# First scores inside the last projection job of three attention layers, and three moved steps

## What is computed

```python
# layer 1 (moba_attention; one block of 256 keys, so it is causal softmax attention, 8 heads)
proj = h @ w_in                       # 10 column blocks of 512, the last four through a sigmoid
p = softmax(q @ k.T * scale, causal); y = p @ v
# layer 4 (odd_mixer, 16 heads)
q, k, v = split(h @ w_qkv, 3); q = rms_norm(q, q_norm); k = rms_norm(k, k_norm)
p = softmax(q @ k.T * scale + bias); y = (p @ v) @ w_out
# layer 6 (fox_mixer, 16 heads)
log_f = log_sigmoid(f + b_f); c = cumsum(log_f)          # the forget sums
p = softmax(q @ k.T * scale + c[q] - c[k], causal); y = ((p @ v) * silu(z)) @ w_out
# layer 7 (nsa_mixer): attention on compressed blocks, then two more branches
p_c = softmax(q @ kc.T * scale); o_c = p_c @ vc          # the compressed weights are p_c
```

## Time and profile before

| What | Value |
|---|---|
| Time, median of 3 runs (lowest to highest) | 2000.18 us (2000.02 to 2001.02) |
| Time of the profiled execution | 1999.24 us |
| Its span | 1997.5 us |
| Mean granted clock of TensorE | 0.996 of 2.4 GHz |
| Busy: PE, PE weight loads, DVE, ACT, POOL | 1933.7, 1592.1, 1522.3, 1272.0, 96.2 us |
| Chain that ended last: PE, DVE, ACT, DMA, issue | 85%, 7%, 4%, 2%, 2% |
| DMA | 535.14 MB, mean 268 GB/s |

### The profile page before, as it was taken

How to read it: one execution, slowest core, us unless ns; L and a number is a source line. 1 busy time by engine, 2 the same in 40 slices (tenths; PEclk the granted TensorE clock), 3 DMA queues, 4 the chain that set the end, 5 groups by cost and what they waited for, 6 DMA issues and landing times.

```text
span 1997.5 us, 26032 instructions
## 1 busy us (share of the span) xinstructions
PE 1933.7 (97%) x9572; PEld 1592.1 (80%) x9572; DVE 1522.3 (76%) x1718; ACT 1272.0 (64%) x1400; POOL 96.2 (5%) x102
## 2 busy tenths in 40 slices
PE   6999999999998999999999999999999989999998
PEld 4887887888887788888888888888888867778876
DVE  7666766544586789989898988989989884467686
ACT  4544676534545677777787777877777765446464
POOL 1000300000000320000000000000000000100001
PEclk9999999999999999999999999999999999999999
DMA  9863645555452599999999999999999995624500
GB/s 366 275 226 120 213 169 191 203 183 189 159 193 82 180 412 367 377 387 365 385 356 392 370 381 376 373 388 358 380 387 370 377 366 169 211 64 149 174 1 32
DMA packets 186269, 535.14 MB, mean 268 GB/s; under 512 B 12609, under 2 KB 23893, under 8 KB 186198
## 3 DMA queue, kind: packets, MB, share of 16 engines
q1 hardware_dynamic: 179952, 518.95, 71.0%
q10 hardware_dynamic: 4422, 8.92, 1.2%
q0 software_dynamic: 1824, 6.31, 1.1%
HBM read 521.02 MB, written 13.12 MB: 267 GB/s over the span
## 4 chain that ended last, share of the span: by engine, by line
PE 85%; DVE 7%; ACT 4%; DMA 2%; issue 2%; ACTq 0%; DVEq 0%; SPq 0%
PE bank L467 25%; PE bank L469 24%; PE bank L468 24%; DVE WL L1193 3%; ACT WH L1189 2%; PE bank L671 1%; DMA ring<-in_od_we_down 1%; PE bank L660 1%; PE bank L2772 1%; DVE P L1177 1%; PE bank L375 1%; PE bank L439 1%; PE bank L686 1%; PE bank L684 1%; DMA ring<-in_od_we_up 1%
## 5 line engine op out<-in xcount | busy, mean ns | idle before, releaser
L1193 DVE TENSOR_TENSOR WL<-ring,WH 128x2048 fp32r<-128x2048 f32 x475 | 1073.0, 2279 | 257.6 <-ACT WH L1189 254.0
L1189 ACT ACTIVATE WH<-ring 128x2048 fp32r<-128x2048 f32 x475 | 901.8, 1912 | 351.0 <-PE bank L469 332.0
L467 PE MATMUL bank<-WH,XTH 128*128 128x512 f32 (+1 forms) x1872 | 738.3, 394 | 9.2 <-DVE XTL L396 3.0
L469 PE MATMUL bank<-WH,XTL 128*128 128x512 f32 (+1 forms) x1872 | 727.8, 389 | 0.0
L468 PE MATMUL bank<-WL,XTH 128*128 128x512 f32 (+1 forms) x1872 | 727.1, 388 | 0.0
L467 PEld LDWEIGHTS bank<-WH,XTH 128*128 128x128 f32 x1872 | 352.6, 188 | 95.0 <-DVE WL L1193 14.7
L469 PEld LDWEIGHTS bank<-WH,XTL 128*128 128x128 f32 x1872 | 352.5, 188 | 73.5
L468 PEld LDWEIGHTS bank<-WL,XTH 128*128 128x128 f32 x1872 | 353.0, 189 | 68.8 <-issue 0.2
L467 PE MATMUL bank<-WH,HTH 128*128 128x512 f32 (+1 forms) x568 | 219.9, 387 | 1.4 <-DVE WL L1193 1.1
L469 PE MATMUL bank<-WH,HTL 128*128 128x512 f32 (+1 forms) x568 | 217.9, 384 | 0.0
L468 PE MATMUL bank<-WL,HTH 128*128 128x512 f32 (+1 forms) x568 | 217.6, 383 | 0.0
(11 more groups left out here) (450 smaller groups left out, 1382.2 us busy)
## 6 DMA issues: line engine op xcount, KB each, us to landing
ring<-in_od_we_gate SPq DMA_DIRECT2D x112, 1024.0 KB, 7.2
ring<-in_od_we_up SPq DMA_DIRECT2D x112, 1024.0 KB, 8.5
ring<-in_od_we_down SPq DMA_DIRECT2D x112, 1024.0 KB, 8.4
ring<-in_w_in SPq DMA_DIRECT2D x20, 1024.0 KB, 6.8
ring<-in_fox_w_in SPq DMA_DIRECT2D x16, 1024.0 KB, 6.6
ring<-in_nsa_w_in SPq DMA_DIRECT2D x14, 1024.0 KB, 5.0
ring<-in_w_ada SPq DMA_DIRECT2D x12, 1024.0 KB, 10.3
ring<-in_ev_w_in SPq DMA_DIRECT2D x12, 1024.0 KB, 5.2
```

The costliest lines, as they stand in the source:

```text
L467: nc.tensor.matmul(out, x[0], wt[0][:, k, :], start=start, stop=False, skip_group_check=check)
L469: return nc.tensor.matmul(out, x[1], wt[0][:, k, :], start=False, stop=stop, skip_group_check=check)
L1189: nc.scalar.activation(wh, slot_ap(n, nk, width), ACT.Copy).then_inc(hi_made, 1)
L1193: nc.vector.tensor_tensor(wl, slot_ap(n, nk, width), wh.bitcast(F32), ALU.subtract).then_inc(lo_made, 1)
```

## The change

- `Project` gets `shift`, which turns the four banks by two; P1 uses it. Job 9 then writes banks 0 and 1, job 8 banks 2 and 3.
- In layers 1, 4 and 6 the scores of pair 0 are issued between the two halves of the last job (keys (9, 1, 0), (5, 1, 0) and (8, 1, 0)). DVE does `highest` of units 0 and 1 behind the splits of the last job and ahead of its wait for the eviction; ACT does the exponentials of units 0 and 1 ahead of the eviction of the last job. PE's wait for all evictions moves: in layers 1 and 6 behind the scores of pair 2 (scores of pair 1 wait for the last but one job), in layer 4 behind the turns of units 0 and 1, ahead of the scores of pair 1.
- Layer 4: queries are turned ahead of the second half of job 4, keys inside the first half of job 5 (ahead of token tile 1). ACT evicts the query turns and takes the root for the keys ahead of the eviction of job 4, and evicts the key turns and rounds the router weights behind it; DVE evicts the query turns ahead of the norm of the keys. `roped` is raised once more, so later waits on it count one more. In A4 the transposes for the output product come one step sooner (`soon=1`).
- Layer 6: DVE copies the forget sums ahead of its wait for the eviction of job 4 instead of behind it.
- Layer 7: the turn of the compressed weights moves from ahead of the second half of job 7 to ahead of that half's token tile 1.

```diff
@@ -472,15 +472,15 @@
...
-    def __init__(self, jobs, lhs, scale=None, narrow=None, tall=None, by_parts=0):
-        self.jobs, self.lhs, self.scale, self.by_parts = jobs, lhs, scale, by_parts
+    def __init__(self, jobs, lhs, scale=None, narrow=None, tall=None, by_parts=0, shift=0):
+        self.jobs, self.lhs, self.scale, self.by_parts, self.shift = jobs, lhs, scale, by_parts, shift
...
-        return bank[4 + tt if c == 2 and self.by_parts == 3 else (2 * c + tt) % 4]
+        return bank[4 + tt if c == 2 and self.by_parts == 3 else (2 * (c + self.shift) + tt) % 4]
@@ -686,23 +686,28 @@
...
-    def pe(self, pe, early=None, first=0):
+    def pe(self, pe, early=None, first=0, entered=None, ended=None, soon=0, turned_pairs=0):
...
         for p in range(N + 2):
+            if entered and p == 1:
+                entered()
...
                 self.scores(pe, p)
+            if ended and p == 2:
+                ended()
             for a in range(2):
-                if 1 <= p <= N:
+                if 1 + turned_pairs <= p <= N:
...
                     self.weigh(pe, 2 * (p - 2) + a)
-                if early and (p, a) in ((N, 1), (N + 1, 0)):
-                    if p == N:
+                step = 2 * (p - N) + a - 1 + soon
+                if early and step in (0, 1):
+                    if step == 0:
                         pe.wait_ge(maxed, self.u + 2 * N)
-                    early(1 - a)
-
-    def act(self, act):
-        for i in range(len(self.units)):
+                    early(step)
+
+    def act(self, act, first=0, end=None):
+        for i in range(first, len(self.units) if end is None else end):
@@ -734,7 +739,7 @@
...
-    def dve(self, dve, early=None, gate=None):
+    def dve(self, dve, early=None, gate=None, first=0):
@@ -744,7 +749,7 @@
...
             for a in range(2):
-                if p < N:
+                if first <= p < N:
@@ -813,7 +818,7 @@
...
 P1 = Project([(c_in1[i], 512, pcol(in1_order[i], 512), {512: ACT.Silu, 2560: ACT.Silu}.get(in1_order[i], ACT.Copy)
-               if in1_order[i] < 3072 else ACT.Sigmoid) for i in range(10)], xt, by_parts=3)
+               if in1_order[i] < 3072 else ACT.Sigmoid) for i in range(10)], xt, by_parts=3, shift=1)
@@ -1697,8 +1702,8 @@
...
     act.dma_start(GRP, t["w_pool_grp"][0].rearrange("g c d -> c g d")).then_inc(band_in, 16)
-    P1.act(act, {3: lambda: TQ1.act(act)})
-    A1.act(act)
+    P1.act(act, {3: lambda: TQ1.act(act)}, {9: lambda: A1.act(act, 0, 2)})
+    A1.act(act, 2)
@@ -1819,11 +1824,14 @@
...
     scaled(act, "act_root")
-    P4.act(act, {2: lambda: roots(act, stat[:, 16:48]), 4: lambda: roots(act, stat[:, 16:48])})
-    TQ4.act(act)
-    act.wait_ge(rw_in, 16)
-    nc.scalar.activation(RH, RW[:, :, :], ACT.Copy).then_inc(r_hi, 1)
-    A4.act(act)
+    def keys4():
+        TQ4.act(act, 4)
+        act.wait_ge(rw_in, 16)
+        nc.scalar.activation(RH, RW[:, :, :], ACT.Copy).then_inc(r_hi, 1)
+
+    P4.act(act, {2: lambda: roots(act, stat[:, 16:48]), 4: keys4},
+           {4: lambda: (roots(act, stat[:, 16:48]), TQ4.act(act, 0, 4)), 5: lambda: A4.act(act, 0, 2)})
+    A4.act(act, 2)
@@ -1885,8 +1893,8 @@
...
     P6.act(act, {2: forget, 4: lambda: TQ6.act(act, 0, 4), 5: lambda: TQ6.act(act, 4)},
-           {2: lambda: P6.narrow_act(act, 1)})
-    A6.act(act)
+           {2: lambda: P6.narrow_act(act, 1), 8: lambda: A6.act(act, 0, 2)})
+    A6.act(act, 2)
@@ -2040,8 +2048,10 @@
...
     dve.sem_inc(gate_ready, 1)
+    for i in range(2):
+        A1.highest(dve, i)
     P1.wait(dve)
-    A1.dve(dve, lambda: TY1.dve(dve))
+    A1.dve(dve, lambda: TY1.dve(dve), first=1)
@@ -2167,15 +2177,20 @@
...
     rms(dve)
-    P4.dve(dve, {1: lambda: head_sums(dve, 0), 2: lambda: head_norm(dve, 0, [(0, 16, "od_q")]),
-                 3: lambda: head_sums(dve, 1024), 4: lambda: head_norm(dve, 1024, [(0, 16, "od_k")])})
-    dve.sem_inc(roped, 1)
-    P4.wait(dve)
-    TQ4.dve(dve)
+    def heads4(c0, name):
+        head_norm(dve, c0, [(0, 16, name)])
+        dve.sem_inc(roped, 1)
+
+    P4.dve(dve, {1: lambda: head_sums(dve, 0), 2: lambda: heads4(0, "od_q"), 3: lambda: head_sums(dve, 1024),
+                 4: lambda: TQ4.dve(dve, 4)},
+           {4: lambda: (TQ4.dve(dve, 0, 4), heads4(1024, "od_k"))})
...
     dve.wait_ge(r_lo, 1)
-    A4.dve(dve, lambda: TO4[0].dve(dve))
+    for i in range(2):
+        A4.highest(dve, i)
+    P4.wait(dve)
+    A4.dve(dve, lambda: TO4[0].dve(dve), first=1)
@@ -2323,11 +2338,13 @@
...
         nc.vector.tensor_copy(FC, bank[4][0:16, 0:S]).then_inc(f_cc, 1)
-        TQ6.dve(dve, 0, 4)
-
-    P6.dve(dve, {1: forget_in, 2: forget, 4: forget_sums, 5: lambda: TQ6.dve(dve, 4)})
+
+    P6.dve(dve, {1: forget_in, 2: forget, 4: lambda: TQ6.dve(dve, 0, 4), 5: lambda: TQ6.dve(dve, 4)},
+           {4: forget_sums})
+    for i in range(2):
+        A6.highest(dve, i)
     P6.wait(dve)
-    A6.dve(dve, lambda: TO6[0].dve(dve), lambda: gate6(dve))
+    A6.dve(dve, lambda: TO6[0].dve(dve), lambda: gate6(dve), 1)
@@ -2560,11 +2577,15 @@
...
-    P1.pe(pe, T1, {2: other_columns, (2, 0, 1): last_columns, 4: heads1, 6: differences, 8: mixed_groups})
-    P1.wait(pe)
-    TQ1.wait(pe)
+    def first_scores1():
+        TQ1.wait(pe)
+        pe.wait_ge(d_copied, 1)
+        A1.scores(pe, 0)
+
+    P1.pe(pe, T1, {2: other_columns, (2, 0, 1): last_columns, 4: heads1, 6: differences, 8: mixed_groups, (9, 1, 0): first_scores1})
     pe.wait_ge(y_gated, 1)
-    A1.pe(pe, lambda a: TY1.pe(pe, first=a, end=a + 1))
+    A1.pe(pe, lambda a: TY1.pe(pe, first=a, end=a + 1), first=1,
+          entered=lambda: pe.wait_ge(proj_act, P1.ba + 9), ended=lambda: P1.wait(pe))
@@ -2700,12 +2721,25 @@
...
-    P4.pe(pe, T4, late=late_tiles(pe, 2, T4))
-    P4.wait(pe)
-    pe.wait_ge(roped, 3)
-    TQ4.pe(pe)
-    TQ4.wait(pe)
-    A4.pe(pe, lambda a: (pe.wait_ge(grouped, A4.g + 1), TO4[0].pe(pe, first=a, end=a + 1)))
+    def queries4():
+        pe.wait_ge(roped, 3)
+        TQ4.pe(pe, 0, 4)
+
+    def keys4():
+        pe.wait_ge(roped, 4)
+        TQ4.pe(pe, 4)
+
+    def first_scores4():
+        TQ4.wait(pe)
+        A4.scores(pe, 0)
+    def entered4():
+        A4.turn(pe, 0)
+        A4.turn(pe, 1)
+        P4.wait(pe)
+
+    P4.pe(pe, T4, {(4, 1): queries4, (5, 0, 1): keys4, (5, 1, 0): first_scores4}, late=late_tiles(pe, 2, T4))
+    A4.pe(pe, lambda a: (pe.wait_ge(grouped, A4.g + 1), TO4[0].pe(pe, first=a, end=a + 1)), first=1,
+          entered=entered4, turned_pairs=1, soon=1)
@@ -2831,11 +2865,14 @@
...
-    P6.pe(pe, T6, {(2, 1): lambda: P6.turn_columns(pe, 1), 4: forget_sums, 5: queries6, 6: keys6}, late6)
-    P6.wait(pe)
-    TQ6.wait(pe)
-    pe.wait_ge(const_set, 11)
-    A6.pe(pe, lambda a: (pe.wait_ge(g6, 1), TO6[0].pe(pe, first=a, end=a + 1)))
+    def first_scores6():
+        TQ6.wait(pe)
+        pe.wait_ge(const_set, 11)
+        A6.scores(pe, 0)
+
+    P6.pe(pe, T6, {(2, 1): lambda: P6.turn_columns(pe, 1), 4: forget_sums, 5: queries6, 6: keys6, (8, 1, 0): first_scores6}, late6)
+    A6.pe(pe, lambda a: (pe.wait_ge(g6, 1), TO6[0].pe(pe, first=a, end=a + 1)), first=1,
+          entered=lambda: pe.wait_ge(proj_act, P6.ba + 8), ended=lambda: P6.wait(pe))
@@ -2843,7 +2880,7 @@
...
     def raw_blocks():
-        pe.wait_ge(roped, 4)
+        pe.wait_ge(roped, 5)
@@ -2880,7 +2917,7 @@
...
     def turn_queries():
-        pe.wait_ge(roped, 5)
+        pe.wait_ge(roped, 6)
@@ -2913,8 +2950,8 @@
...
                    6: lambda: (turn_hidden(1), turn_compressed()),
-                   (6, 1): lambda: (P7.turn_columns(pe, 2), compressed_scores(), second_layer(1)), (7, 1): turn_weights}, late7)
-    pe.wait_ge(roped, 6)
+                   (6, 1): lambda: (P7.turn_columns(pe, 2), compressed_scores(), second_layer(1)), (7, 1, 1): turn_weights}, late7)
+    pe.wait_ge(roped, 7)
```

## The result

| Kernel | Median | Lowest to highest | Executions |
|---|---|---|---|
| before, beside the changed kernel | 2000.60 us | 1999.63 to 2003.99 | 6 |
| changed | 2008.51 us | 2006.35 to 2013.65 | 6 |

The changed kernel takes 1.004 of the time of the one before (95% interval 1.0029 to 1.0051). Forecast was 1996.2; it came out 8 slower than the kernel before, 12 above the forecast. The profiled execution took 2008.61 (span 2006.8, mean granted clock 0.989) against 1999.24 (1997.5, 0.996). The first part of the profile's page shows PE busy 12 us longer, with the same 9572 matmuls.

A forecast was written before the change was run, and what follows sets the result against it. TensorE, busy 97% of the span, was taken as the bound. Gains 0.15 + 0.2 + 1.85 + 0.9 + 1.9 - 0.2 (changeovers) = 4.8, less 0.85 for the clock, 4.0: from 2000.18 to 1996.2 us; range 1993.0 to 1998.9.

The forecast's parts named there:

- A1, third unit: Layer one: early scores mostly eaten by ACT's table changes; third unit turned at 157.7 against 157.81, gain 0.1 to 0.2.
- A4, third unit: Layer four: new waits replace the old ones; third unit turned at 611.05 against 611.00, nothing gained.
- A4, output product: End of layer four's attention: turns one step sooner save about 0.35 of a 0.97 wait; layer four 0.2 in all.
- P6, sums' wait: Layer six: PE's 1.80 wait for DVE's copy of the forget sums goes; gain 1.85, bounds 1.6 and 2.0.
- A6, third unit: Layer six: with early scores, third unit turned at 1749.3 against 1750.22; gain 0.9, bounds 0.3 and 1.3.
- P7, last keys: Layer seven: keys' turns start at 1907.95 instead of 1909.86 after a 2.4 wait; gain 1.9.
- table drain: Rival: each ACT table change in layers one and six costs a further 1.38; 2000.9, chance 0.04.
- queue behind the keys' wait: Layer four: the wait of 2.0 for normed keys in job 5 might start a queue; bound -1.
- 0.85 for a possible clock fall in A1: Layer one: charge for half clock after the new 2.7 wait, taken between bounds 0 and 1.7.
- the price of 1.7: Cost of one clock fall: PE at granted clock 0.52 for 3.5 us, read in layer seven's projection.
- 2.37 kept the clock: Layer seven: one earlier wait of 2.37 kept 2.4 GHz, so the new 2.4 wait was charged nothing (bound 1.7).
- The clock falls at each new wait: Rival: falls in A1, job 5, A6 and P7 at 1.7 apiece, 4.8 - 6.8; 2002.2, chance 0.03.

The follow-up runs named there:

- first1_alone: Kernel before with layer one's part alone (scores of pair 0 inside job 9, banks shifted, exponentials ahead of the Sigmoid); 2009.3 us, ratio 1.0044.
- p7_alone: Kernel before with layer seven's step alone, the turn of the compressed weights one token tile later; 2001.6 us, ratio 0.9995.
- after_filled: Changed kernel with idle products in its new waits in A1, A6, ahead of layer seven's last keys and at A7's start; 1997.0 us, ratio 0.9974.
- sums_alone: Kernel before with only layer six's copy of the forget sums moved; 2000.2 us, ratio 1.0001.
- layer4_alone: Kernel before with layer four's part of the change alone; 2001.4 us, ratio 1.0017.
- before_longer_wait: Kernel before with one more activation of another function ahead of A1's first exponential, lengthening PE's wait there; 2003.6 us, ratio 1.0019.
- after_layer1_back: Changed kernel with layer one's part undone; 2003.8 us, ratio 1.0015.
- before_filled: Kernel before with idle products in its own waits in A1, A6, between the two tiles of compressed weights and at A7's start; 2000.8 us, ratio 0.9994.
- best: Changed kernel without layer one's part, idle products in A1, A6, at the experts' end, ahead of layer seven's last keys, at A7's start; 1997.7 us, ratio 0.9977.

## Why the prediction was wrong, point by point

**The order of the work: right, to a few tenths.** In the times of before, with the shift that stands ahead of each step taken off (2.9 in layer four, 3.1 and then 1.2 in layer six, 1.7 in layer seven):

| Step | Forecast | Profile after | Gain, forecast and found |
|---|---|---|---|
| A1, third unit | 157.7 | 157.62 | 0.15, 0.2 |
| A4, third unit | 611.05 | 611.5 | -0.05, -0.5 |
| A4, output product | | 633.7 | 0.2, 0.1 |
| P6, sums' wait | gone | gone | 1.85, 1.95 |
| A6, third unit | 1749.3 | 1749.25 | 0.9, 0.95 |
| P7, last keys | 1907.95 | 1908.0 | 1.9, 1.9 |

The sum found is 5.1 (A4's third unit is within its output product), forecast 4.8 with changeovers; all executions together give 4.3 ± 0.4 at full clock. A4's third unit comes 0.5 late, behind the copy of a turn that the forecast had no wait for, and its end makes that good. No table drain, no queue behind the keys' wait.

**The term that failed: "0.85 for a possible clock fall in A1", and the price of 1.7 under it.** The price was read from one place, where PE ran a projection when the clock fell, and was carried to an attention. There a fall can last much longer, and nearly half of it is lost: 20.6 us in A7, and in A1 7 in the changed kernel's own profile, 14 in that of first1_alone, 20.6 in that of p7_alone. That is 3 to 10 in place of 1.7. A6's fall, 3.5 us long, cost no more than the price. The chance was too low as well. The bound "2.37 kept the clock" was one execution; in others, the profile of after_filled for one, the clock falls behind that very wait.

**The rival that came true is the slower one, with a price far too small.** "The clock falls at each new wait" was given 0.03 and 2002.2. In A1 it falls in all three profiles that have this wait unfilled, in A6 in three of four; in job 5 and P7 it did not in the profile, and A7, where it cost most, was in no rival, since the change has no instruction there; the profiles above point at layer six's part for it. The range was built from sums of 1.7 and could not reach 2008.

**What was taken for fixed and isn't.** Three executions within 1 us of each other looked like a kernel with one time. About one execution of six takes some 8 us more, and that these three held none of them was luck.

## What to carry to other kernels

Where TensorE is 97% busy, ask of every moved wait not only how long it is but what PE does behind it: here waits of 1.2 to 2.5 us ahead of small transposes and scores were followed by falls that cost up to 10 us, while the falls inside P7's projection cost 1.7 to 3.4. Three waits with 2.8 in sum lost less than one of 2.54, though the order around them differed too. A handful of products that nobody reads, put into the wait, kept the clock up there and delayed nothing. Before a price of the clock is taken from a trace, look at the mean granted clock of many executions: span times clock tells an order of work from its falls, without waiting for an execution that has none.

## What the runs showed of the hardware

- **The granted clock falls by chance behind waits of 1.2 us**, in unchanged code: the profiles of sums_alone and p7_alone have A1 at 1.2 GHz for 20.5 us behind two waits of 1.2 and one of 0.33, that of before has it at 2.4 GHz throughout. With the falls that every profile has at its start and end, an execution of the kernel before loses from 6 to 26 us to half clock, 11.3 in the mean. The Trainium skill (TensorE: Matmul & The Clock Gate, What's actually happening) says of the ramp at a kernel's start that the number of slow matmuls differs from run to run of the same kernel, and that its penalty is under 1% of a typical span. Here what the whole kernel loses differs from run to run as well; it is 0.6% before the change and 1.1% after.
- **How long a fall lasts differs, with PE shown busy all the while.** In projections 3.5 us and 6.9 (sums_alone at 1908.5, layer4_alone at 1907.9), in attentions anything from 3.5 to 20.6: A1's lasts 3.5 in before_longer_wait, 7 in the changed kernel, 13.8 in first1_alone, 20.6 in p7_alone. Those of more than 7 us began in an attention, but for one of 10.4 at the start of layer one (after_layer1_back, 43.9). The small products of an attention may be the reason, but that was not tried, and they can't be all of it: A7's fall in the changed kernel ends at 1939.9, with the same work going on to 1973. What ends a fall stays open.
- **Idle products of 0.18 us each hold the clock** at 2.4 GHz through A1 in each profile of a kernel that fills its wait there, and no execution of after_filled, before_filled or best takes 2005 or more.
